# One layer of a hybrid attention and experts model: residual rows from transposed columns, two weight pieces held outside the ring

## The chip, the cores and the metric

The kernel runs on one core of a Trainium2 chip. The metric is device time in microseconds for one call, the median of several executions. The core has TensorE (PE) for matmuls, VectorE (DVE), ScalarE (ACT), GpSimd (POOL) and SyncE (SP), which here only issues DMAs.

## The reference

The input is 256 tokens of width 2048 in float32. After the projections, an attention, an mLSTM and an output projection, the layer ends like this:

```python
h = layer_norm(DN_ALPHA * h + mix @ w_out[l], ln1_g[l], ln1_b[l])
ff = hier_moe(h, w_grp[l], b_grp[l], w_exp[l], b_exp[l], w_gate[l], w_up[l], w_down[l])
ple = (p[l] @ w_ple[l]) * jax.nn.sigmoid(h @ w_ple_gate[l])
h = layer_norm(DN_ALPHA * h + ff + ple, ln2_g[l], ln2_b[l])
```

DN_ALPHA is 2 ** 0.25. There are 16 experts of hidden width 512 in 4 groups of 4; each token uses 2 experts of one group. The product h @ w_ple_gate is 256 x 2048 by 2048 x 2048.

## The kernel before

Up to about 934 us the kernel runs the projections. Each weight is split into a high and a low part, and four SBUF quarters of 1 MB are filled by SP. Then comes the first layer norm. DVE writes the normalised rows z (without gain and bias) into RES. PE transposes them (`row_turn`, L846), and ACT and DVE write the columns hT, with gain and bias, as h1T. The rows z also go to the output buffer in DRAM (L401), for a branch on overflow that is not taken here.

From about 965 us the experts run, in pairs: eight pairs, n = 0 to 7. `up(n)` (L999) has eight slots. A slot uses two loads of 1 MB, one for each expert of the pair, even slots from w_gate and odd ones from w_up (`up_slot`, L990, eight matmuls of 64 stationary columns by 512). `down(n)` (L1051) has four slots of two loads of w_down (`down_slot`, L1043). ORDER (L62) is up(0), up(1), down(0), up(2), down(1), up(3) and so on. PE also does, between slots: the gathers of the tokens of the next group (in up(0) and in down(0), down(2), down(4)), the turn of the hidden rows after slot 2 (`turn_pair`), and the scatters of pair n-2 after slots 2 and 5.

The product with w_ple_gate is cut into 16 chunks of 512 rows by 512 columns. The first (`ple_early`, loaded at L371) is held outside the ring and worked in up(0). The other 15, numbered i = 0 to 14, stand at the slots that CHUNKS_IN (L66) lists: after that slot, `ple_chunk` (L915) runs eight matmuls on one load of 1 MB. ACT copies the first chunk of four into ple_sig, DVE adds the others (`ple_added`, L2212).

All these weights come through moe_ring, 8 slots of 1 MB. The list LOADS (L84) holds its loads in the order of their use, each slot's two and behind them the chunk's one, 207 in all. SP issues them in this order (`ring_load`, L386). Load m goes into slot m % 8, and from m = 8 on SP waits for the use of load m - 8 (L393). So a load can't be issued while the ring is full, and nothing behind it either.

The residual rows are DN_ALPHA * h. Here ACT loads the gain and the bias of the first norm as broadcast rows (ln_g, ln_b, 1 MB each; at L1432 and L1433), scales both by ALPHA (L1590, L1591), and DVE multiplies and adds them to the rows of RES (`residual`, L2069 to L2076). ACT and DVE wait for that (res_ready) before the first sums of down(0).

Of the kernel before, what the change touches and what calls it, by code (L numbers as in the profile page):

```python
# [64 lines left out]

CHUNKS_IN = (("up", 1, 4), ("up", 2, 2), ("up", 2, 5), ("up", 3, 2), ("up", 3, 5), ("up", 4, 2), ("up", 4, 5),  # L66
             ("up", 5, 2), ("up", 5, 5), ("up", 6, 2), ("up", 6, 5), ("down", 5, 1), ("up", 7, 2), ("up", 7, 5),
             ("down", 6, 1))
SPLIT_FROM = 9
CHUNK_OF = {at: i for i, at in enumerate(CHUNKS_IN)}  # L70

# [13 lines left out]
for item in ORDER:  # L85
    for slot in range(SLOTS_OF[item[0]]):
        LOADS += [item + (slot, 0), item + (slot, 1)]
        if item + (slot,) in CHUNK_OF:
            LOADS.append(("ple", CHUNK_OF[item + (slot,)], 0, 0))
# [45 lines left out]
def build(nc, x, p, w_in, kv_norm, w_ukv, m_i_bias, m_f_bias, w_proj_a, w_proj_m, w_out, ln1_g, ln1_b,  # L135
          w_grp, b_grp, w_exp, b_exp, w_gate, w_up, w_down, w_ple, w_ple_gate, ln2_g, ln2_b, out):
    with ExitStack() as ctx:
# [21 lines left out]
        EW = at("ple_early", [EARLY, D], Z0 + 16384)  # L159
        lng = at("ln_g", [D], Z0)  # L160
        lnb = at("ln_b", [D], Z0 + 8192)
        ygh = at("yg_hi", [4, NC], Z0, F32R)
# [78 lines left out]
        def tiny(n):  # L241
# [49 lines left out]
        n2_diag, n2_mm, n2_out = sem("norm_diagonal"), sem("norm_mm"), sem("norm_out")  # L291
        z_ready, z_T, hT_act, hT_dve, rows_scaled = (sem("z_ready"), sem("z_T"), sem("hT_act"), sem("hT_dve"),
                                                     sem("rows_scaled"))
        wr_zero, r_part = sem("wr_zero"), sem("r_part")
        h1_hi, h1_lo, res_gain, res_ready = sem("h1_hi"), sem("h1_lo"), sem("res_gain"), sem("res_ready")
        ple_in, pT_mm, pT_c, pp_mm, pp_c = sem("ple_in"), sem("pT_mm"), sem("pT_copied"), sem("pp_mm"), sem("pp_copied")
        split_hi, split_lo = sem("turned_or_gate_hi"), sem("turned_or_gate_lo")
        z_moved = sem("z_rows_moved")
        ple_sig, ple_done, ple_ev = sem("ple_sig"), sem("ple_done"), sem("ple_evac")
        early_in, early_used = [sem(f"early_in{s}") for s in range(EARLY)], sem("early_used")  # L300
        r_in, r_row, r_mm, r_exp, r_log = sem("r_in"), sem("r_row"), sem("r_mm"), sem("r_exp"), sem("r_log")
# [25 lines left out]
        def _(sp):  # L327
# [42 lines left out]
            for q in range(EARLY):  # L370
                sp.dma_start(EW[:, EARLY - 1 - q, :].rearrange("p (t n) -> p t n", t=4),  # L371
                             ple_v[:, 4 * q:4 * q + 4, 0:NC]).then_inc(early_in[q], 16)
            load_tiles(T_OUT + 2, 2, w_out[0], 2 * NC)
            gate_v = w_gate.rearrange("l e (p t) f -> p (l e) t f", p=P)
            up_v = w_up.rearrange("l e (p t) f -> p (l e) t f", p=P)
# [140 lines left out]
        def _(pe):  # L516
# [398 lines left out]
            def ple_chunk(at, b):  # L915

                i = CHUNK_OF[at]
                pe.wait_ge(ple_ev, i + 1)
                if i < SPLIT_FROM:
                    ple_rows(landed_load(("ple", i, 0, 0)), b, (i + EARLY) % 4, True, True).then_inc(ring_used, 1)  # L920
                else:
                    split_rows(i, b).then_inc(ring_used, 1)
# [67 lines left out]
            def up_slot(w, i, b0, e0):  # L990
# [6 lines left out]
                return last  # L997

            def up(n):  # L999

                b, other = 2 * (n % 2), 2 * ((n + 1) % 2)
                if n and n % 2 == 0:
                    pe.wait_ge(g_act, 8 + 4 * (n // 2))
                    pe.wait_ge(g_dve, 4 * (n // 2))
                if n:
                    pe.wait_ge(ple_ev, max(chunks_in("up", n - 1) + chunks_in("down", n - 2), default=-1) + 2)
                for i in range(UP_SLOTS):
                    w = landed_pair("up", n, i)
                    if n == 0 and i % 2 == 0:
                        pe.wait_ge(g_act, i + 2)  # L1010
                    up_slot(w, i, b, 2 * (n % 2)).then_inc(ring_used, 2)
                    if n == 0 and i in (1, 3):
                        if i == 1:
                            pe.wait_ge(combined, 1)
                            weight_table(5, selT_mm)
                        first_pairs(i // 2 + 2)
                    if n == 0 and i == 6:
                        ple_rows(EW[:, 0, :], 2, 0, True, True, (1, 2, 3)).then_inc(early_used, 1)
                    if i == 2:
                        if n:  # L1020
# [174 lines left out]
        def _(ac):  # L1195
# [230 lines left out]
            def before(h):  # L1426
                if h < 3:
                    mix_turned(h + 3)
                if h == 4:
                    product(T_MIX + 15)  # L1430
                    ac.dma_start(RES[:], x[0].rearrange("(a p) k -> p a k", p=P)).then_inc(x2_in, 16)
                    ac.dma_start(lng[:], ln1_g[0:1, :].to_broadcast([P, D])).then_inc(ln_in, 16)  # L1432
                    ac.dma_start(lnb[:], ln1_b[0:1, :].to_broadcast([P, D])).then_inc(ln_in, 16)  # L1433
                    ac.dma_start(lgc, ln1_g[0].rearrange("(q t) -> q t", t=KT)).then_inc(ln_in, 16)
                    ac.dma_start(lbc, ln1_b[0].rearrange("(q t) -> q t", t=KT)).then_inc(ln_in, 16)
                    ac.dma_start(wple[:], w_ple[0].rearrange("(k p) n -> p k n", p=P)).then_inc(ple_in, 16)
                if h == 7:
                    mix_turned(6)
# [32 lines left out]
            for n in range(4):  # L1471
                pp_copy(n)
            ac.wait_ge(ln_in, 64)
            for i in range(0, 8, 2):
# [110 lines left out]
            for i in range(8):  # L1585
# [3 lines left out]
                gained(i, B[6 + i % 2]).then_inc(g_act, 1)  # L1589
            fn(lng[:], lng[:], ACT.Copy, scale=ALPHA).then_inc(rows_scaled, 1)  # L1590
            fn(lnb[:], lnb[:], ACT.Copy, scale=ALPHA).then_inc(rows_scaled, 1)  # L1591
            ple_started(0, 2)
            ac.wait_ge(r_all, 1)
            over = ac.value_load(flag[0:1, 0:1], min_val=0, max_val=1)
            for kind, n in ORDER:
                if kind == "up":
                    if n:
                        hidden_turned(n - 1)
                    if n >= 6:
                        gate_high(10 if n == 6 else 13)  # L1600
# [66 lines left out]
        def _(dv):  # L1667
# [400 lines left out]

            def residual(a):  # L2069

                dv.wait_ge(h1_lo, 4)
                dv.wait_ge(rows_scaled, 2)
                dv.wait_ge(z_moved, 16)
                v.tensor_tensor(RES[:, a, :], RES[:, a, :], lng[:], ALU.mult).then_inc(res_gain, 1)
                dv.wait_ge(res_gain, a + 1)
                v.tensor_tensor(RES[:, a, :], RES[:, a, :], lnb[:], ALU.add).then_inc(res_ready, 1)  # L2076

            moments(1, link)
            for a in range(NT):
                v.tensor_scalar(RES[:, a, :], RES[:, a, :], mv2[:, 2 * a:2 * a + 1], rstd[:, a:a + 1], ALU.subtract,  # L2080
                                ALU.mult).then_inc(z_ready, 1)
            dv.wait_ge(ln_in, 64)
            for i in range(1, 8, 2):
# [118 lines left out]
            def ple_part(j):  # L2202
# [3 lines left out]
                if j == 0:  # L2206
                    dv.wait_ge(pp_c, 8)
                    dv.wait_ge(res_ready, 2)
                link(v.tensor_tensor(psg[:], psg[:], pp[:, :, c], ALU.mult))
                v.tensor_tensor(RES[:, :, c], RES[:, :, c], psg[:], ALU.add).then_inc(ple_done, 1)  # L2210

            def ple_added(i, b):  # L2212

                dv.wait_ge(ring_used, LOAD_AT["ple", i, 0, 0] + 1)
                dv.wait_ge(ple_ev, i + 1)
# [28 lines left out]
            def add(n, c, b0, blocks=range(NT)):  # L2244

                if (n, c) == (0, 0):
                    dv.wait_ge(res_ready, 2)
                for a in blocks:
# [43 lines left out]
            overflow()  # L2292
            residual(0)
            residual(1)
            dv.wait_ge(r_all, 1)
            over = dv.value_load(flag[0:1, 0:1], min_val=0, max_val=1)
            for kind, n in ORDER[:-1]:
                for slot in range(SLOTS_OF[kind]):
                    if kind == "up" and n >= 2 and slot in (2, 5):
                        if parts_done((kind, n, slot)):  # L2300
# [146 lines left out]
```

## Time and profile before

| | us |
|---|---|
| median of 3 runs | 1511.32 |
| lowest and highest | 1510.46 and 1512.3 |
| the profiled execution | 1512.64 |
| its span, first to last instruction | 1511.1 |
| PE busy | 1481.9 (98%) |
| DVE busy | 701.2 (46%) |
| ACT busy | 513.5 (34%) |
| HBM read | 391.71 MB |

A busy PE is not PE at its peak, since the ends of matmuls are modelled. The chain that ended last gives PE 92% and DMA 4% of the span. An `L` number is a line of the kernel before. In a timeline, instructions of one kind in a row are merged, with their count behind an x; a bracket gives the idle time before and what ended it.

### The profile page before, as it was taken

To read this page: it belongs to the slowest core of one execution; us is meant where nothing else is said; L and a number is where in the kernel's file an instruction comes from. 1 tells how busy PE (TensorE), PEld (TensorE's weight loads), DVE (VectorE), ACT (ScalarE), POOL (GpSimd) and SP (SyncE) were. 2 spreads that over 40 slices of the span, in tenths; PEclk is the share of its full clock that TensorE was granted. 3 is DMA by queue.
4 is the path that set the end of the run, shared out by engine and by line. 5 is a ranking of instruction groups with operands and counts; after the bars stand their busy time and mean duration, and the time that the engine had idled before them with its cause. 6 is when DMAs were issued, how large, how long until landed. Compare 5 with 4: busy or idle time off the path is not lost.

```text
span 1511.1 us, 17027 instructions
## 1 busy us (share of the span) xinstructions
PE 1481.9 (98%) x6708; PEld 1012.9 (67%) x6708; DVE 701.2 (46%) x960; ACT 513.5 (34%) x690; POOL 55.1 (4%) x64
## 2 busy tenths in 40 slices
PE   9999999999999999999999999999999998999998
PEld 7887788888878888888888887534434443454443
DVE  5546665457746555454454655531221231143336
ACT  4444444454545443444444433521000200031111
POOL 0000000043300000000000000000000000000000
PEclk9999999999999999999999999999999999999999
DMA  8654555544444556555555876599999999999994
GB/s 307 198 173 161 167 168 195 192 151 159 139 141 138 176 172 202 192 191 189 193 193 191 312 263 228 202 418 421 416 416 417 396 389 421 419 388 419 416 403 177
DMA packets 133006, 397.00 MB, mean 263 GB/s; under 512 B 13248, under 2 KB 15936, under 8 KB 108096
## 3 DMA queue, kind: packets, MB, share of 16 engines
q1 hardware_dynamic: 124352, 388.65, 69.5%
q10 hardware_dynamic: 8576, 7.28, 1.5%
q8 instruction: 52, 0.85, 0.2%
q14 instruction: 26, 0.21, 0.0%
HBM read 391.71 MB, written 4.19 MB: 262 GB/s over the span
## 4 chain that ended last, share of the span: by engine, by line
PE 92%; DMA 4%; DVE 1%; issue 1%; ACT 1%; POOL 0%; SPq 0%; DVEq 0%; ACTq 0%; POOLq 0%
PE bank L525 19%; PE bank L526 19%; PE bank L530 19%; PE bank L995 12%; PE bank L1047 5%; PE bank L911 4%; DMA moe_ring<-in_w_gate_dram 2%; PE bank L959 2%; DMA moe_ring<-in_w_ple_gate_dram 2%; PE bank L1090 1%; PE bank L1075 1%; PE bank L1091 1%; PE bank L933 1%; PE bank L935 1%; PE bank L934 1%; DMA moe_ring<-in_w_down_dram 1%
## 5 line engine op out<-in xcount | busy, mean ns | idle before, releaser
L1681 DVE TENSOR_TENSOR w_lo<-w_ring,w_hi 128x1024 fp32r<-128x1024 f32 (+1 forms) x312 | 382.1, 1227 | 299.5 <-ACT w_hi L1211 298.4
L1211 ACT ACTIVATE w_hi<-w_ring 128x1024 fp32r<-128x1024 f32 (+1 forms) x312 | 327.3, 1051 | 308.0 <-PE bank L530 308.0
L525 PE MATMUL bank<-w_hi,xT_hi 128*128 128x512 f32 (+1 forms) x864 | 346.6, 401 | 1.7 <-ACT w_hi L1211 1.7
L526 PE MATMUL bank<-w_hi,xT_lo 128*128 128x512 f32 (+1 forms) x864 | 335.0, 388 | 0.0
L995 PE MATMUL bank<-moe_ring,xg 128*64 128x512 f32 x1024 | 225.9, 594 | 8.6 <-DMA moe_ring<-in_w_gate_dram 6.0
L530 PE MATMUL bank<-w_lo,xT_hi 128*128 128x512 f32 (+1 forms) x864 | 229.2, 387 | 0.0
L525 PEld LDWEIGHTS bank<-w_hi,xT_hi 128*128 128x128 f32 x864 | 162.3, 188 | 38.1 <-issue 6.7
L526 PEld LDWEIGHTS bank<-w_hi,xT_lo 128*128 128x128 f32 x864 | 162.5, 188 | 32.3 <-issue 1.9
L530 PEld LDWEIGHTS bank<-w_lo,xT_hi 128*128 128x128 f32 x864 | 161.6, 188 | 33.1
L995 PEld LDWEIGHTS bank<-moe_ring,xg 128*64 128x64 f32 x1024 | 72.7, 137 | 154.9 <-issue 154.5
L1047 PE MATMUL bank<-moe_ring,moe_hiddenT 128*64 128x512 f32 x448 | 100.0, 595 | 1.4 <-DMA moe_ring<-in_w_down_dram 1.4
L2254 DVE TENSOR_TENSOR res<-res,bank 128x512 f32<-128x512 f32 x62 | 38.5, 682 | 104.1 <-issue 80.0
L1047 PEld LDWEIGHTS bank<-moe_ring,moe_hiddenT 128*64 128x64 f32 x448 | 31.4, 137 | 61.2 <-issue 60.0
L911 PE MATMUL bank<-moe_ring,h1T 128*128 128x512 f32 x144 | 63.4, 593 | 0.0
L2217 DVE TENSOR_TENSOR ple_sig<-bank,ple_sig 128x512 f32<-128x512 f32 x24 | 15.5, 687 | 80.5 <-PE bank L911 57.1
L525 PE MATMUL bank<-w_hi,ymT_hi 128*128 128x512 f32 x128 | 50.4, 394 | 0.0
L525 PE MATMUL bank<-w_hi,mixT_hi 128*128 128x512 f32 x128 | 50.1, 391 | 0.0
L526 PE MATMUL bank<-w_hi,ymT_lo 128*128 128x512 f32 x128 | 49.9, 390 | 0.0
L526 PE MATMUL bank<-w_hi,mixT_lo 128*128 128x512 f32 x128 | 49.8, 389 | 0.0
L525 PE MATMUL bank<-w_hi,yaT_hi 128*128 128x512 f32 x128 | 49.8, 389 | 0.0
L526 PE MATMUL bank<-w_hi,yaT_lo 128*128 128x512 f32 x128 | 49.8, 389 | 0.0
L911 PEld LDWEIGHTS bank<-moe_ring,h1T 128*128 128x128 f32 x144 | 27.2, 190 | 31.6 <-issue 31.0
(297 smaller groups left out, 1390.9 us busy)
## 6 DMA issues: line engine op xcount, KB each, us to landing
w_ring<-in_w_in_dram SPq DMA_DIRECT2D x103, 1024.0 KB, 5.0
moe_ring<-in_w_gate_dram SPq DMA_DIRECT2D x64, 1024.0 KB, 9.7
moe_ring<-in_w_up_dram SPq DMA_DIRECT2D x64, 1024.0 KB, 10.4
moe_ring<-in_w_down_dram SPq DMA_DIRECT2D x64, 1024.0 KB, 10.3
w_ring<-in_w_proj_a_dram SPq DMA_DIRECT2D x16, 1024.0 KB, 5.0
w_ring<-in_w_proj_m_dram SPq DMA_DIRECT2D x16, 1024.0 KB, 5.0
w_ring<-in_w_out_dram SPq DMA_DIRECT2D x16, 1024.0 KB, 5.2
moe_ring<-in_w_ple_gate_dram SPq DMA_DIRECT2D x15, 1024.0 KB, 13.0
```

What stands on the lines that cost most here:

```text
L525: mm(b, lh(k, m), WH[:, s, kk, 0:width], start=start and kk == 0, stop=False)
L526: mm(b, ll(k, m), WH[:, s, kk, 0:width], start=False, stop=False)
L530: last = mm(b, lh(k, m), WL[:, s, kk, 0:width], start=False, stop=stop and kk == 1)
L911: ins = mm(B[b + a][:, :], hT[:, k, a * P:a * P + P], w[:, t * NC:t * NC + NC], start=first and t == 0, stop=last and t == 3)
L933: mm(B[b + a][:, :], hTh[:, k, r], GH[:, j % 2, c], start=t == 0, stop=False)
L959: last = mm(b[:, kk * TOK:kk * TOK + TOK], src[:, a, 2 * i + kk, :], selg[:, a, :], start=part == 0 and a == 0, stop=part == 1 and a == 1)
L995: last = mm(B[b0 + i % 2][CAP * e:CAP * e + CAP, :], xg[:, k, (e0 + e) * CAP:(e0 + e) * CAP + CAP], w[e][:, t * NC:t * NC + NC], start=k = ...
L1047: last = mm(B[4 + c][CAP * e:CAP * e + CAP, :], src[:, k, CAP * e:CAP * e + CAP], w[e][:, c * NC:c * NC + NC], start=k == 0, stop=k == 3)
L1211: fn(WH[:, h % 4, :, 0:width], W32[:, h // 2, 2 * (h % 2):2 * (h % 2) + 2, 0:width], ACT.Copy).then_inc(hi_ready, 1)
L1681: v.tensor_tensor(WL[:, h % 4, :, 0:width], W32[:, h // 2, 2 * (h % 2):2 * (h % 2) + 2, 0:width], WH[:, h % 4, :, 0:width].bitcast(F32), A ...
L2217: last = v.tensor_tensor(psg[:, a, :], B[b + a][:, :], psg[:, a, :], ALU.add)
L2254: v.tensor_tensor(r, r, B[b0 + a][:, :], ALU.add).then_inc(y_add, 1)
```

## The change

The residual rows are no longer made from the rows z. PE transposes the columns hT back, eight turns of four 128x128 blocks into banks 6 and 7, two turns after each of the slots 0, 1, 3 and 4 of up(1). ACT evacuates the even turns and DVE the odd ones, with the factor ALPHA, into the strided columns of RES. The broadcast rows, their loads and their scalings go. Their room holds the pieces of chunks 0 and 1, which SP loads behind the last tile of w_out and ahead of the ring's first load. The ring carries 205 loads. Chunk 0 moves from up(1) slot 4 to up(1) slot 2, chunk 1 from up(2) slot 2 to up(1) slot 4. A core of the diff:

```diff
-CHUNKS_IN = (("up", 1, 4), ("up", 2, 2), ("up", 2, 5), ("up", 3, 2), ("up", 3, 5), ("up", 4, 2), ("up", 4, 5),
+CHUNKS_IN = (("up", 1, 2), ("up", 1, 4), ("up", 2, 5), ("up", 3, 2), ("up", 3, 5), ("up", 4, 2), ("up", 4, 5),
...
+AHEAD = 2
...
-        if item + (slot,) in CHUNK_OF:
+        if CHUNK_OF.get(item + (slot,), -1) >= AHEAD:
             LOADS.append(("ple", CHUNK_OF[item + (slot,)], 0, 0))
...
-        lng = at("ln_g", [D], Z0)
-        lnb = at("ln_b", [D], Z0 + 8192)
+        AW = at("ple_ahead", [AHEAD, D], Z0)
...
             load_tiles(T_OUT + 2, 2, w_out[0], 2 * NC)
+            for q in range(EARLY, EARLY + AHEAD):
+                sp.dma_start(AW[:, q - EARLY, :].rearrange("p (t n) -> p t n", t=4),
+                             ple_v[:, 4 * q:4 * q + 4, 0:NC]).then_inc(early_in[q], 16)
...
-                if i < SPLIT_FROM:
+                if i < AHEAD:
+                    pe.wait_ge(early_in[EARLY + i], 16)
+                    ple_rows(AW[:, i, :], b, i + EARLY, True, True).then_inc(early_used, 1)
+                elif i < SPLIT_FROM:
...
+            def residual_turn(r):
+
+                pe.wait_ge(res_act if r % 2 == 0 else res_dve, r // 2)
+                for k in range(4):
+                    t, a = 4 * (r // 2) + k, r % 2
+                    last = nc.tensor.transpose(B[6 + a][:, k * P:k * P + P], hT[:, t, a * P:a * P + P], ident[:])
+                last.then_inc(res_T, 1)
...
                     up_slot(w, i, b, 2 * (n % 2)).then_inc(ring_used, 2)
+                    if n == 1 and i in (0, 1, 3, 4):
+                        for r in range(2):
+                            residual_turn(2 * (0, 1, 3, 4).index(i) + r)
...
                 if n:
                     pe.wait_ge(y_add, 2 * CHUNKS * n)
+                else:
+                    pe.wait_ge(res_act, 4)
+                    pe.wait_ge(res_dve, 4)
...
-                    ac.dma_start(lng[:], ln1_g[0:1, :].to_broadcast([P, D])).then_inc(ln_in, 16)
-                    ac.dma_start(lnb[:], ln1_b[0:1, :].to_broadcast([P, D])).then_inc(ln_in, 16)
...
-            fn(lng[:], lng[:], ACT.Copy, scale=ALPHA).then_inc(rows_scaled, 1)
-            fn(lnb[:], lnb[:], ACT.Copy, scale=ALPHA).then_inc(rows_scaled, 1)
...
+            def residual(r):
+
+                ac.wait_ge(h1_lo, 4)
+                ac.wait_ge(z_moved, 16)
+                ac.wait_ge(res_T, r + 1)
+                t = 4 * (r // 2)
+                fn(RES[:, r % 2, :].rearrange("p (q t) -> p t q", t=KT)[:, t:t + 4, :], four(6 + r % 2), ACT.Copy,
+                   scale=ALPHA).then_inc(res_act, 1)
+
             for kind, n in ORDER:
                 if kind == "up":
+                    if n == 1:
+                        residual(0)
+                        residual(2)
                     if n:
                         hidden_turned(n - 1)
+                    if n == 1:
+                        residual(4)
+                        residual(6)
...
                     if n == 0:
-                        ac.wait_ge(res_ready, NT)
+                        ac.wait_ge(early_used, EARLY + AHEAD)
...
-            def residual(a):
-
-                dv.wait_ge(h1_lo, 4)
-                dv.wait_ge(rows_scaled, 2)
-                dv.wait_ge(z_moved, 16)
-                v.tensor_tensor(RES[:, a, :], RES[:, a, :], lng[:], ALU.mult).then_inc(res_gain, 1)
-                dv.wait_ge(res_gain, a + 1)
-                v.tensor_tensor(RES[:, a, :], RES[:, a, :], lnb[:], ALU.add).then_inc(res_ready, 1)
...
             def ple_added(i, b):
 
-                dv.wait_ge(ring_used, LOAD_AT["ple", i, 0, 0] + 1)
+                if i < AHEAD:
+                    dv.wait_ge(early_used, EARLY + i + 1)
+                else:
+                    dv.wait_ge(ring_used, LOAD_AT["ple", i, 0, 0] + 1)
...
+            def residual(r):
+
+                dv.wait_ge(h1_lo, 4)
+                dv.wait_ge(z_moved, 16)
+                dv.wait_ge(res_T, r + 1)
+                t = 4 * (r // 2)
+                v.tensor_scalar(RES[:, r % 2, :].rearrange("p (q t) -> p t q", t=KT)[:, t:t + 4, :], four(6 + r % 2),
+                                ALPHA, None, ALU.mult).then_inc(res_dve, 1)
+
             for kind, n in ORDER[:-1]:
                 for slot in range(SLOTS_OF[kind]):
+                    if kind == "up" and n == 1 and slot in (0, 1, 3, 4):
+                        residual(2 * (0, 1, 3, 4).index(slot) + 1)
```

Every wait on ln_in is 32 and no longer 64, and the first `add` and the first `ple_part` wait for res_act and res_dve at 4 in place of res_ready at 2.

## Rows read from the trace of the kernel before

**Rows 1.** The page, 40 slices of the span: PE, DMA and GB/s.
```profile
PE   9999999999999999999999999999999998999998
...
DMA  8654555544444556555555876599999999999994
...
GB/s 307 198 173 161 167 168 195 192 151 159 139 141 138 176 172 202 192 191 189 193 193 191 312 263 228 202 418 421 416 416 417 396 389 421 419 388 419 416 403 177
```

**Rows 2.** Windows of the second stage: busy us (x count), PEclk, DMA share, GB/s.
```profile
970.00:1040.00 70.00, 69.10 (x308) 26.61 (x306) 14.54 (x18) 12.05 (x18) 0.00 (x0) 1.00 1.01 416
...
1040.00:1075.00 35.00, 34.71 (x189) 17.12 (x189) 6.47 (x12) 7.08 (x15) 0.00 (x0) 1.00 1.02 418
...
1190.00:1210.00 20.00, 19.87 (x102) 8.27 (x99) 4.47 (x8) 3.09 (x7) 0.00 (x0) 1.00 0.94 373
...
1220.00:1250.00 30.00, 30.00 (x124) 11.39 (x122) 9.37 (x19) 1.65 (x2) 0.00 (x0) 1.00 0.98 383
...
965.00:1485.00 520.00, 504.31 (x2239) 221.91 (x2239) 136.82 (x217) 75.40 (x124) 0.00 (x0) 1.00 1.00 406
```

**Rows 3.** Waits of PE after 850: us in total, times, longest us.
```profile
PE bank L995 <- DMA moe_ring<-in_w_gate_dram: 6.0, 5, 1.3
...
PE bank L995 <- DMA moe_ring<-in_w_up_dram: 2.6, 2, 1.3
...
PE bank L1047 <- DMA moe_ring<-in_w_down_dram: 1.4, 2, 0.9
```

**Rows 4.** Timeline of PE, 994 to 1060: start us, us, instructions merged.
```profile
999.90 13.95 PE L995 MATMUL bank<-moe_ring,xg 128*64 128x512 f32 x64
...
1013.78 0.66 PE L1036 MATMUL bank<-ident,moe_hidden 128*128 128x128 f32 x4
...
1014.37 7.09 PE L995 MATMUL bank<-moe_ring,xg 128*64 128x512 f32 x32
...
1021.39 7.13 PE L911 MATMUL bank<-moe_ring,h1T 128*128 128x512 f32 x16
...
1028.45 10.52 PE L995 MATMUL bank<-moe_ring,xg 128*64 128x512 f32 x48
...
1039.88 3.65 PE L1047 MATMUL bank<-moe_ring,moe_hiddenT 128*64 128x512 f32 x16 [0.90 <-DMA moe_ring<-in_w_down_dram]
...
1046.92 3.65 PE L1047 MATMUL bank<-moe_ring,moe_hiddenT 128*64 128x512 f32 x16
```

**Rows 5.** Timeline of SP's queue: first ring loads, first ones after a release.
```profile
909.12 7.47 SPq L394 DMA_DIRECT2D moe_ring<-in_w_gate_dram  x2
...
968.66 0.80 SPq L394 DMA_DIRECT2D moe_ring<-in_w_gate_dram  x2
```

**Rows 6.** Windows (columns as in Rows 2) before the experts' stage.
```profile
905.00:935.00 30.00, 30.00 (x134) 24.59 (x133) 13.24 (x14) 8.08 (x9) 0.53 (x1) 1.00 0.59 180
...
940.00:945.00 5.00, 4.70 (x33) 3.63 (x32) 3.66 (x7) 3.40 (x8) 0.00 (x0) 1.00 1.06 415
...
955.00:970.00 15.00, 14.29 (x79) 8.70 (x79) 11.80 (x33) 9.60 (x15) 0.00 (x0) 1.00 0.03 6
```

**Rows 7.** Groups by line and form, 880 to 1040: busy us, mean ns, idle before.
```profile
L858 PE MATMUL bank<-ident,res 128*128 128x128 f32 x32 | 4.0, 283 | 0.3 <-DVE res L2080 0.3
...
L2076 DVE TENSOR_TENSOR res<-res,ln_b 128x2048 f32<-128x2048 f32 x2 | 4.6, 2292 | 0.1
...
L2091 DVE TENSOR_TENSOR h_lo<-res,h_hi 128x512 fp32r<-128x512 f32 x8 | 8.0, 1086 | 0.0
...
L1571 ACT ACTIVATE moe_hiddenT<-bank 128x512 f32<-128x512 f32 x1 | 0.6, 597 | 11.5 <-PE bank L1036 11.5
```

**Rows 8.** Timeline of PE at the start of up(3), 1125 to 1136.
```profile
1125.60 3.65 PE L995 MATMUL bank<-moe_ring,xg 128*64 128x512 f32 x16 [1.21 <-DMA moe_ring<-in_w_gate_dram]
1130.57 3.65 PE L995 MATMUL bank<-moe_ring,xg 128*64 128x512 f32 x16 [1.32 <-DMA moe_ring<-in_w_up_dram]
1135.57 3.65 PE L995 MATMUL bank<-moe_ring,xg 128*64 128x512 f32 x16 [1.34 <-DMA moe_ring<-in_w_gate_dram]
```

More of the change, by code:

```diff
@@ L291, in build @@
         n2_diag, n2_mm, n2_out = sem("norm_diagonal"), sem("norm_mm"), sem("norm_out")
-        z_ready, z_T, hT_act, hT_dve, rows_scaled = (sem("z_ready"), sem("z_T"), sem("hT_act"), sem("hT_dve"),
-                                                     sem("rows_scaled"))
+        z_ready, z_T, hT_act, hT_dve, res_T = (sem("z_ready"), sem("z_T"), sem("hT_act"), sem("hT_dve"),
+                                               sem("res_T"))
         wr_zero, r_part = sem("wr_zero"), sem("r_part")
-        h1_hi, h1_lo, res_gain, res_ready = sem("h1_hi"), sem("h1_lo"), sem("res_gain"), sem("res_ready")
+        h1_hi, h1_lo, res_act, res_dve = sem("h1_hi"), sem("h1_lo"), sem("res_act"), sem("res_dve")
         ple_in, pT_mm, pT_c, pp_mm, pp_c = sem("ple_in"), sem("pT_mm"), sem("pT_copied"), sem("pp_mm"), sem("pp_copied")
@@ L299, in build @@
         ple_sig, ple_done, ple_ev = sem("ple_sig"), sem("ple_done"), sem("ple_evac")
-        early_in, early_used = [sem(f"early_in{s}") for s in range(EARLY)], sem("early_used")
+        early_in, early_used = [sem(f"early_in{s}") for s in range(EARLY + AHEAD)], sem("early_used")
         r_in, r_row, r_mm, r_exp, r_log = sem("r_in"), sem("r_row"), sem("r_mm"), sem("r_exp"), sem("r_log")
@@ L1472, in _ @@
                 pp_copy(n)
-            ac.wait_ge(ln_in, 64)
+            ac.wait_ge(ln_in, 32)
             for i in range(0, 8, 2):
@@ L2081, in _ @@
                                 ALU.mult).then_inc(z_ready, 1)
-            dv.wait_ge(ln_in, 64)
+            dv.wait_ge(ln_in, 32)
             for i in range(1, 8, 2):
@@ L2207, in ple_part @@
                     dv.wait_ge(pp_c, 8)
-                    dv.wait_ge(res_ready, 2)
+                    dv.wait_ge(res_act, 4)
+                    dv.wait_ge(res_dve, 4)
                 link(v.tensor_tensor(psg[:], psg[:], pp[:, :, c], ALU.mult))
@@ L2246, in add @@
                 if (n, c) == (0, 0):
-                    dv.wait_ge(res_ready, 2)
+                    dv.wait_ge(res_act, 4)
+                    dv.wait_ge(res_dve, 4)
                 for a in blocks:
@@ L2292, in _ @@
             overflow()
-            residual(0)
-            residual(1)
             dv.wait_ge(r_all, 1)
             over = dv.value_load(flag[0:1, 0:1], min_val=0, max_val=1)
+            def residual(r):
[5 more added lines that the diff above has]
+                                ALPHA, None, ALU.mult).then_inc(res_dve, 1)
             for kind, n in ORDER[:-1]:
                 for slot in range(SLOTS_OF[kind]):
+                    if kind == "up" and n == 1 and slot in (0, 1, 3, 4):
+                        residual(2 * (0, 1, 3, 4).index(slot) + 1)
                     if kind == "up" and n >= 2 and slot in (2, 5):
```

## The prediction

> **What bounds the kernel now.** I read the page's slices first. PE is busy in nearly every slice of the span. DMA is moderate up to the 26th slice and then sits at 9 tenths and about 418 GB/s until the end [rows 1]. So the span has two stages, and the change touches the second, the experts' stage from 965 us on. The windows say how tight it is: in 965 to 1485 the DMA engines are busy for 1.00 of the time and PE for 504.3 of 520 us, at clock 1.00 [rows 2]. Neither has spare room. What passes between them is the ring of 8 loads of 1 MB, where load m is issued only when load m-8 has been used (L393). A look at the waits shows PE short of ring loads for 6.0 + 2.6 + 1.4 = 10.0 us in all [rows 3]. The DMA is short of free slots elsewhere: it falls to 0.94 in 1190 to 1210 and to 0.98 in 1220 to 1250 [rows 2]. The reader is to see a system bound by turns. A pair slot (two loads) costs PE 13.95/4 = 3.49 us [rows 4] and the DMA twice 1.049 MB at 418 GB/s, that is 2 x 2.51 = 5.02 us. PE's other work (chunks, gathers, scatters) needs few loads and lets the DMA catch up. If too much of it stands together, the ring is full and the DMA idles; idle DMA time is lost for good, because the rest of the stage needs the DMA at 1.00.
>
> **The edits, part by part.**
>
> *Two ring loads go.* The ple pieces 0 and 1 are now loaded ahead. The ring carries two loads fewer: 2 x 2.51 = 5.0 us less DMA in the stage. They are issued on SP behind w_out's last tile and ahead of the ring's first load, which before was issued at 909.12 [rows 5]. In 905 to 935 the DMA share is 0.59, so 0.41 x 30 = 12.3 us are free against the 5.0 that come in, and in 955 to 970 the DMA stands still again (0.03) [rows 6]. The first ring loads are used at 965. I cost this at nothing; without that cover it would be 5.0 us. The two broadcast loads on ACT's queue (2 MB, around 880 us) go; PE has no wait there, so nothing is gained.
>
> *Residual rows.* Gone are four DVE operations of 128x2048, two of each of two lines, and two ACT scalings. One line's pair took 4.6 us, so the four are 9.2 us [rows 7]. All of it lies beside PE work and nothing on PE waits for it. Added are four evacuations on ACT and four on DVE of 128x512, between 0.60 us (a plain ACT evacuation) and 1.09 us (a DVE one with strided rows) [rows 7]. PE comes back to the same bank only after at least one slot of 3.49 us, so they are hidden. Cover gone, each costs up to 1.1 us. The new waits of ACT and DVE in up(1) stand ahead of the sigmoid, the hidden turn and the chunk sums; these are due one slot or more later. SP issues no DMA behind them.
>
> *Turns on PE.* Eight turns of four transposes enter up(1), two after each of slots 0, 1, 3 and 4. Thirty-two transposes in a row took 4.0 us [rows 7], four alone 0.6 us (1013.78 to 1014.37) [rows 4]. So all cost between 4.0 and 8 x 0.6 = 4.8 us. I take 4.4 (1.1 a visit), since they come in eights. They are on PE's path.
>
> The Trainium skill (TensorE: Matmul & The Clock Gate, Part 4: PE-mode transpose) gives about 275 ns for a 128x128 transpose in a kernel's context. Estimated from that page the turns would be 32 x 0.275 = 8.8 us, and the sum below about 4.4 us worse. The row with 32 of them speaks for 4.0 us, since they overlap.
>
> *Chunks move.* Chunk 0 moves from slot 4 to slot 2 of up(1), and chunk 1 from slot 2 of up(2) to slot 4 of up(1). A chunk costs PE 7.0 us (1021.39 to 1028.45) [rows 4]. Both now stand in up(1) with no load of their own in the ring. This is the part that decides.
>
> **The sum, by the ring.** I follow PE through up(1) from the timeline [rows 4]. Up(0) ends where four slots from 999.90 began, plus one: 1003.5. With 3.5 us a slot, 1.1 a visit, 0.6 for the turn of the hidden rows and 7.0 a chunk, slots 0 to 2 end at 1007.0, 1011.6 and 1016.2. The hidden turn and chunk 0 run to 1023.8. Slots 3 and 4 end at 1027.3 and 1031.9. The visit and chunk 1 run to 1040.0, and slots 5, 6, 7 end at 1043.5, 1047.0, 1050.5. Before, down(0) began at 1039.88, after a wait of 0.90 [rows 4]; so PE is 10.6 us late there.
>
> Now the DMA. Its stream starts about 970.4, some 1.5 us after the first release of 968.66 [rows 5], and takes 2.51 us a load. The release at 1016.2 has freed 22 loads, done at 970.4 + 22 x 2.51 = 1025.6. The next release is at 1027.3, transfers resume at 1028.8: 3.2 us lost. Slots 3 and 4 free four loads, done at 1038.8. The next release is 1043.5, resumed at 1045.0: 6.2 us lost. Slots 5 to 7 and the first three of down(0) (7.06 us each with a gather part, as from 1039.88 to 1046.92 [rows 4]) free 12 loads, done at 1075.1. The last slot of down(0) ends at 1075.3, resumed at 1076.8: 1.7 us lost. Together 11.1 us are lost, where before 970 to 1075 shows 1.01 and 1.02 with nothing lost [rows 2]. From there on up(2) has no chunk at slot 2, and its releases come faster than 5 us until slot 5, so the DMA runs through.
>
> Net: 11.1 lost less 5.0 saved is 6.1 us late at the loads of up(3). Before, PE waited there three times for them, and the third slot began at 1135.57 [rows 8]. PE's own path is only 4.4 + 0.1 a switch for 4 visits, less the wait of 0.90, about 3.9 us later there, so the DMA is what comes last: PE waits again, and for some 2 us more. From there both kernels do the same work in the same order, and the ring fills and empties as before: the delay is carried to the end. The turns count one for one in it, because they stand ahead of the releases. I take 6.0.
>
> The profiled execution took 1512.64 us with a span of 1511.1, that is 1.5 us around it, and the median of the three runs shown is 1511.32. A delay of 6.0 on the span adds the same to each: the forecast is 1511.3 + 6.0 = 1517.3 us.
>
> **The rivals.**
>
> 1. *The ring never runs full (faster).* If the DMA alone bounded the stage, two loads fewer would give 5.0 us back: 1506.3. For it speaks the DMA share of 1.00 over 520 us [rows 2]. Against it speaks the depth of the ring: 8 loads are 20 us of DMA, and in up(1) PE now spends 23.8 us (1016.2 to 1040.0) in which it frees only four loads. It would take a stream 5 us behind the one I worked out.
> [...]
>
> 2. *The turns go into PE's waits (no change).* PE's waits for loads up to the third slot of up(3) are 0.90 + 1.21 + 1.32 + 1.34 = 4.8 us [rows 4, 8]. If the DMA came 5 us earlier, the 4.4 of turns would fill them: -0.4 us, 1510.9. This needs the lost DMA time of up(1) to be under some 5 us.
>
> 3. *PE alone sets the delay (slower, less).* The DMA's lost time is smaller than 9 us and PE's extra path of 3.9 us shows: 1515.2.
>
> 4. *The turns cost more.* If each visit waits for an evacuation (up to 1.1 us), or the granted clock falls to the lower level of 1.2 GHz around them, up(1) grows by 4.4 us and the delay by the same: 1521.7. Against: in 940 to 945, which holds most of the 32 transposes of that row, the clock is 1.00 [rows 6].
> The Trainium skill (TensorE: Matmul & The Clock Gate, Part 4: PE-mode transpose) says that transposes don't count as PE work for the clock gate; here they make up 1.1 us between stretches of matmuls, and no row shows a fall after them.
>
> **Chances.** Forecast (delay of 4.5 to 8 us) 0.62; rival 3 (3 to 4.5) 0.12; rival 4 (over 8) 0.09; rival 2 (within 3 us) 0.11; rival 1, or another gain, 0.06. A measurement of this kernel can tell about 0.2% from no change, 3.0 us. So slower 0.83, same 0.11, faster 0.06. The range leaves out rivals 1 and 2 and the far end of rival 4: from 1511.3 + 2.7 = 1514.0 to 1511.3 + 9.2 = 1520.5.
>
> **What would show it.** In the profile after: PE's transposes of up(1) near 4.4 us in all; down(0) starting near 1050.5; the DMA share falling well below 1 in about 1025 to 1029 and 1039 to 1045; no wait of PE at the start of down(0); three or four waits of PE at the start of up(3), each near 1.3 us, with its third slot near 1141.6; and from there the same picture 6 us later. It would be wrong if the DMA is at 1.00 all through up(1), if the start of up(3) is not later than before, or if a new wait stands between a turn and its evacuation.

## The result and the profile after

| | before | changed |
|---|---|---|
| median of the timed runs, us | 1511.8 (6 runs) | 1517.14 (6 runs) |
| lowest and highest | 1509.52 and 1514.79 | 1516.18 and 1519.29 |
| profiled execution, us | 1512.64 | 1517.15 |
| its span | 1511.1 | 1515.6 |

The ratio is 1.0032, with a 95% interval of 1.0017 to 1.0046: the changed kernel is 0.3% slower, 5.3 us by the medians. 1517.3 was forecast. Further down, two of the ten executions of e7 (3904 and 5273 us) are left out of its numbers, and its trace is that of a second run, e7b.

The page of the changed kernel, the lines that answer to [rows 1] (span; 40 slices of PE, of the DMA engines, and the GB/s moved):

```profile
span 1515.6 us, 17099 instructions
...
PE   9999999999999999999999999999989998999997
...
DMA  9654555554443555555565867597999999999994
...
GB/s 308 199 182 148 169 174 193 187 167 139 140 159 124 188 167 194 194 194 194 194 194 192 314 216 273 217 421 316 402 422 416 386 398 421 418 389 419 416 403 175
```

PE is as full as before. The DMA is not: the 28th slice, which begins at 27 x 37.9 = 1023 us, has fallen to 7 tenths and 316 GB/s. That slice covers the second half of up(1) and the start of down(0).

PE's timeline there, as in [rows 4] (start us, us, instructions merged, count):

```profile
1006.12 1.09 PE L1010 MATMUL bank<-ident,h1T 128*128 128x128 f32 x8
...
1007.15 3.65 PE L1001 MATMUL bank<-moe_ring,xg 128*64 128x512 f32 x16
...
1010.73 1.09 PE L1010 MATMUL bank<-ident,h1T 128*128 128x128 f32 x8
...
1015.34 0.66 PE L1053 MATMUL bank<-ident,moe_hidden 128*128 128x128 f32 x4
...
1015.83 7.03 PE L914 MATMUL bank<-ple_ahead,h1T 128*128 128x512 f32 x16
...
1026.38 1.09 PE L1010 MATMUL bank<-ident,h1T 128*128 128x128 f32 x8
...
1030.99 1.09 PE L1010 MATMUL bank<-ident,h1T 128*128 128x128 f32 x8
...
1031.92 7.03 PE L914 MATMUL bank<-ple_ahead,h1T 128*128 128x512 f32 x16
...
1038.88 10.52 PE L1001 MATMUL bank<-moe_ring,xg 128*64 128x512 f32 x48
...
1049.23 3.60 PE L1064 MATMUL bank<-moe_ring,moe_hiddenT 128*64 128x512 f32 x16
```

L1010 are the turns, L914 the chunks, L1053 the turn of the hidden rows, L1064 down(0). Eight transposes take 1.03 us of PE (1006.12 to 1007.15). Chunk 0 stands at 1015.83, chunk 1 at 1031.92. Down(0) begins at 1049.23 and no longer waits for a load; before it began at 1039.88 after a wait [rows 4]. The whole stage began 0.8 us earlier in this profiled execution. That comes from the first 10 us of the kernel, where the eight transposes that begin at 5.92 took 1.07 us in place of 1.91, in a part that the change doesn't touch.

Windows of 5 us (busy us of PE, PEld, DVE, ACT, POOL with counts, granted clock, DMA share, GB/s):

```profile
1015.00:1020.00 5.00, 5.00 (x16) 2.40 (x15) 0.00 (x0) 0.60 (x1) 0.00 (x0) 1.00 1.02 426
...
1020.00:1025.00 5.00, 5.00 (x19) 1.73 (x18) 1.29 (x2) 0.00 (x0) 0.00 (x0) 1.00 0.89 372
...
1025.00:1030.00 5.00, 5.00 (x28) 2.05 (x26) 1.04 (x1) 1.05 (x1) 0.00 (x0) 1.00 0.51 172
...
1030.00:1035.00 5.00, 5.00 (x22) 2.48 (x19) 1.03 (x1) 1.03 (x1) 0.00 (x0) 1.00 1.02 413
...
1035.00:1040.00 5.00, 5.00 (x16) 1.93 (x16) 1.01 (x2) 0.00 (x0) 0.00 (x0) 1.00 0.63 262
...
1040.00:1045.00 5.00, 5.00 (x26) 1.64 (x24) 0.28 (x1) 0.00 (x0) 0.00 (x0) 1.00 0.27 75
...
1045.00:1050.00 5.00, 5.00 (x26) 1.66 (x24) 1.25 (x2) 0.60 (x1) 0.00 (x0) 1.00 1.01 423
...
1070.00:1075.00 5.00, 5.00 (x26) 1.82 (x26) 1.28 (x3) 1.01 (x3) 0.00 (x0) 1.00 0.80 328
...
1075.00:1080.00 5.00, 5.00 (x26) 1.72 (x24) 2.20 (x4) 1.15 (x3) 0.00 (x0) 1.00 0.98 383
```

Here the lost DMA time can be counted against a full rate of 421 GB/s, which most full windows of 5 us reach within 1%. In 1020 to 1030 it is (49 + 249)/421 x 5 = 3.5 us. In 1035 to 1045 it is (159 + 346)/421 x 5 = 6.0 us, and in 1070 to 1080 (93 + 38)/421 x 5 = 1.6 us. Together 11.1 us, in just the three places of the forecast (3.2, 6.2 and 1.7).

The start of up(3), as in [rows 8]:

```profile
1125.04 3.65 PE L1064 MATMUL bank<-moe_ring,moe_hiddenT 128*64 128x512 f32 x16 [1.31 <-DMA moe_ring<-in_w_down_dram]
...
1130.02 3.65 PE L1001 MATMUL bank<-moe_ring,xg 128*64 128x512 f32 x16 [1.33 <-DMA moe_ring<-in_w_gate_dram]
...
1135.00 3.65 PE L1001 MATMUL bank<-moe_ring,xg 128*64 128x512 f32 x16 [1.32 <-DMA moe_ring<-in_w_up_dram]
...
1139.97 3.65 PE L1001 MATMUL bank<-moe_ring,xg 128*64 128x512 f32 x16 [1.32 <-DMA moe_ring<-in_w_gate_dram]
```

PE waits there four times, 5.3 us in all. Before it waited 0.90 at down(0) and 3.9 in up(3) [rows 4, 8]. To compare stages I count from the start of the second gather group, 962.89 before and 962.10 now, to the third slot of up(3): 172.7 us before, 177.9 now. The delay is 5.2 us, and it is all made by then. From that slot to the last sums (the first L1130 before, L1150 now) it is 355.2 us before and 354.8 now.

### The profile page after: what moved, and what is told of

Its sections match the earlier page's. It is cut to its first block, busy times and chain, and to the rows that moved or that the text cites. A ratio compares the mean times of both kernels' runs of the same rounds, so it can differ in the third digit from the quotient of the medians.

```text
span 1515.6 us, 17099 instructions
## 1 busy us (share of the span) xinstructions
PE 1485.5 (98%) x6740; PEld 1015.3 (67%) x6740; DVE 695.9 (46%) x960; ACT 513.7 (34%) x692; POOL 55.0 (4%) x64
## 4 chain that ended last, share of the span: by engine, by line
PE 93%; DMA 4%; DVE 1%; issue 1%; ACT 1%; POOL 0%; SPq 0%; DVEq 0%; POOLq 0%; ACTq 0%
PE bank L528 19%; PE bank L529 19%; PE bank L533 19%; PE bank L1001 13%; PE bank L1064 5%; PE bank L914 4%; DMA moe_ring<-in_w_gate_dram 2%; PE bank L965 2%; DMA moe_ring<-in_w_ple_gate_dram 2%; PE bank L1110 1%; PE bank L1095 1%; PE bank L1111 1%; PE bank L939 1%; PE bank L940 1%; PE bank L941 1%; PE bank L555 1%
## 5 line engine op out<-in xcount | busy, mean ns | idle before, releaser
L528 PEld LDWEIGHTS bank<-w_hi,xT_hi 128*128 128x128 f32 x864 | 162.3, 188 | 37.9 <-issue 4.6
L1064 PE MATMUL bank<-moe_ring,moe_hiddenT 128*64 128x512 f32 x448 | 100.4, 595 | 1.8 <-DMA moe_ring<-in_w_down_dram 1.7
L1064 PEld LDWEIGHTS bank<-moe_ring,moe_hiddenT 128*64 128x64 f32 x448 | 31.5, 137 | 61.7 <-issue 60.5
L914 PE MATMUL bank<-moe_ring,h1T 128*128 128x512 f32 x112 | 49.2, 592 | 0.0
L2267 DVE TENSOR_TENSOR yg_lo<-bank,yg_hi 128x512 fp32r<-128x512 f32 x32 | 20.1, 682 | 50.4 <-ACT yg_hi L1596 49.9
```

The costliest lines, as they stand in the source:

```text
L528: mm(b, lh(k, m), WH[:, s, kk, 0:width], start=start and kk == 0, stop=False)
L914: ins = mm(B[b + a][:, :], hT[:, k, a * P:a * P + P], w[:, t * NC:t * NC + NC], start=first and t == 0, stop=last and t == 3)
L1064: last = mm(B[4 + c][CAP * e:CAP * e + CAP, :], src[:, k, CAP * e:CAP * e + CAP], w[e][:, c * NC:c * NC + NC], start=k == 0, stop=k == 3)
L2267: v.tensor_tensor(ygl[:, c, :], B[c if n == NP - 1 else 4 + c][:, :], ygh[:, c, :].bitcast(F32), ALU.subtract).then_inc(y_lo, 1)
```

## The experiments

"Stage" is the time from the second gather group to the third slot of up(3) in the profiled execution, less the 172.7 us of before. Each is read from one execution. The other columns are timed runs against the kernel before on the same chip. The ratio isn't the quotient of the two medians; the two differ most for e7 (4.4 us by the ratio, 2.7 by the medians).

| kernel | stage, us | median, us | before, us | ratio and 95% interval |
|---|---|---|---|---|
| changed | +5.2 | 1517.14 | 1511.8 | 1.0032 (1.0017 to 1.0046) |
| e1_no_turns | +0.9 | 1511.87 | 1512.87 | 0.9997 (0.9988 to 1.0006) |
| e2_in_ring | +6.2 | 1518.32 | 1512.87 | 1.0034 (1.0022 to 1.0047) |
| e3_chunks_moved | +1.5 | 1512.37 | 1512.87 | 0.9994 (0.9985 to 1.0003) |
| e4_one_ahead | +5.4 | 1515.94 | 1512.87 | 1.0020 (1.0008 to 1.0031) |
| e7_spare_turns_up1 | +5.3 | 1515.16 | 1512.41 | 1.0029 (1.0016 to 1.0042) |
| e8_spare_turns_down1 | +1.6 | 1512.26 | 1512.41 | 1.0000 (0.9990 to 1.0010) |
| e5_spread | | 1509.4 | 1512.41 | 0.9980 (0.9969 to 0.9991) |
| e9_after_spread | | 1511.36 | 1512.41 | 0.9999 (0.9990 to 1.0008) |
| e10_spread_in_ring | | 1512.4 | 1511.77 | 0.9999 (0.9990 to 1.0008) |

(In the last three a chunk stands inside the stretch, so the stage is not comparable. The stage of e7 is that of e7b, the same kernel.)

### Without the turns: e1_no_turns

The calls of residual_turn and of residual on ACT and DVE are taken out of the changed kernel; DVE's first sums wait for z_moved. DN_ALPHA * h is left out: the sums are added to the rows z.

```diff
-                    if n == 1 and i in (0, 1, 3, 4):
-                        for r in range(2):
-                            residual_turn(2 * (0, 1, 3, 4).index(i) + r)
...
-                    dv.wait_ge(res_act, 4)
-                    dv.wait_ge(res_dve, 4)
+                    dv.wait_ge(z_moved, 16)
```

> The changed kernel without the eight turns of the residual columns and without their evacuations; DN_ALPHA * h is left out, the sums are added to the rows z. Ring theory (a delay is made of DMA time lost while the ring is full, less 5.0 us for two loads saved): slots of up(1) are released earlier by 1.1 us a visit, so lost DMA time falls from about 10 to about 6.7 us (1.0 + 4.0 + 1.7) and the kernel is 1 to 2 us slower than before. Rival (PE's own path alone sets the delay): the two chunks only move past each other, 0 to -1 us against before. Rival (the turns are hidden in PE's waits): still 5 us slower.

The whole loss is gone: 0.9997. In the trace the stage is 0.9 us longer than before. So the turns with their evacuations, of which 4.4 us are PE's, are worth 4.3 us of stage and about 5 us of time, give or take 2.6: they are not hidden. The expected 1 to 2 us slower was not seen in the timed runs; the interval reaches 0.9 us. Why the stage's 0.9 us doesn't show there stays open, as for e3 below.

### The two pieces in the ring again: e2_in_ring

```diff
-AHEAD = 2
+AHEAD = 0
```

> The changed kernel with pieces 0 and 1 loaded through the ring again (207 ring loads), all else as changed. Ring theory: the two loads fall into time in which the DMA stands idle because the ring is full, so nothing changes against the changed kernel: 5 to 6 us slower than before, and the idle DMA time of up(1) is 5 us shorter. Rival (each ring load costs its 2.5 us of DMA in a stage with DMA share 1.00): 5 us more than the changed kernel, 10 us slower than before.

1.0034 against the changed kernel's 1.0032: two loads more cost nothing that the timing shows, and 1.0 us of stage. The windows show where they went (same columns as above):

```profile
1015.00:1035.00 20.00, 20.00 (x79) 8.45 (x76) 3.36 (x4) 2.69 (x3) 0.00 (x0) 1.00 1.01 397
...
1035.00:1055.00 20.00, 20.00 (x90) 7.95 (x89) 2.73 (x4) 1.44 (x4) 0.00 (x0) 1.00 0.90 357
```

The changed kernel has 346 and 297 GB/s in these two windows, this one 397 and 357. That is (51 + 60) GB/s x 20 us = 2.2 MB more: the two loads have filled idle DMA time. The rule that every load counts 2.5 us in a stage with DMA share 1.00 fell.

### Only the chunks moved: e3_chunks_moved

```diff
-CHUNKS_IN = (("up", 1, 4), ("up", 2, 2), ("up", 2, 5),
+CHUNKS_IN = (("up", 1, 2), ("up", 1, 4), ("up", 2, 5),
```

This is the kernel before, with ring loads for all chunks.

> The kernel before with chunks 0 and 1 at up(1) slots 2 and 4, nothing else. Ring theory: PE spends one chunk more in up(1), the ring is full for part of it, and this stage's DMA loses more than the two loads take: 1 to 2 us slower than before. Rival (position is free as long as the order of work is kept): 0.

The stage grew by 1.5 us, as expected, but the timed runs say 0.9994, a miss: no loss of 1 to 2 us. The traces show one thing that goes the other way. Near the end, in the last split chunk, the granted clock fell in the profiled executions of before, changed, e2 and e4, and not in those of e1 and e3. It is worth 1.6 us (the last section has the rows). In the timed runs it doesn't make up the difference: the mean clock that they list is 0.9981 for e3 and 0.9978 for before, and in before's runs 0.001 of it goes with some 0.9 us (1511.65 us on average at 0.999, 1513.32 at 0.997), so this gives 0.2 us. Why the stage's 1.5 us doesn't show in the timed runs stays open.

### One piece ahead, the chunks at their old places: e4_one_ahead

```diff
-CHUNKS_IN = (("up", 1, 2), ("up", 1, 4), ("up", 2, 5),
+CHUNKS_IN = (("up", 1, 4), ("up", 2, 2), ("up", 2, 5),
...
-AHEAD = 2
+AHEAD = 1
```

> The changed kernel with one piece ahead and both chunks at their old places, up(1) slot 4 and up(2) slot 2; the turns stay. Ring theory: 3.5 to 4.5 us slower than before, so the move of the chunks is worth 1 to 2 of the change's 5 us and the turns the rest. Rival (the clump of chunks and turns is all of the cost): 0 to 1 us slower than before.

1.0020, or 3.0 us, with an interval from 1.2 to 4.7 us; the stage is 5.4 us longer, more than the expected 4.5 and as much as the changed kernel's. So, in the stage, the clump of chunks and the second load ahead together carry nothing that the turns don't carry already. The timed runs are 1.8 us below the changed kernel's by the ratios, which their intervals don't tell from nothing. The idle DMA time is only spread differently:

```profile
1035.00:1040.00 5.00, 5.00 (x26) 1.73 (x24) 0.00 (x0) 0.41 (x1) 0.00 (x0) 1.00 0.66 220
...
1065.00:1070.00 5.00, 5.00 (x26) 1.61 (x24) 1.72 (x4) 2.06 (x4) 0.00 (x0) 1.00 0.74 272
```

(220 and 272 GB/s of 421 are 2.4 and 1.8 us lost; 2 us more are lost in 1105 to 1115.)

### The same PE work in two places: e7_spare_turns_up1 and e8_spare_turns_down1

Both are the kernel before with 32 spare transposes of hT into banks that nobody reads. They differ only in the place.

```diff
+            def spare_turn(bank, r):
+                for k in range(4):
+                    t, a = 4 * (r // 2) + k, r % 2
+                    nc.tensor.transpose(B[bank][:, k * P:k * P + P], hT[:, t, a * P:a * P + P], ident[:])
...
                     up_slot(w, i, b, 2 * (n % 2)).then_inc(ring_used, 2)
+                    if n == 1 and i in (0, 1, 3, 4):
+                        for a in range(2):
+                            spare_turn(6 + a, 2 * (0, 1, 3, 4).index(i) + a)
```

and for e8

```diff
                     down_slot(w, k, hidT[:, n % 2]).then_inc(ring_used, 2)
+                    if n == 1:
+                        if k == 0:
+                            pe.wait_ge(ple_ev, max(chunks_in("up", 2)) + 2)
+                        for a in range(2):
+                            spare_turn(2 + a, 2 * k + a)
```

> The kernel before with 32 spare transposes of hT on PE after slots 0, 1, 3 and 4 of up(1), into banks 6 and 7, read by nobody; chunks, loads and residual rows as before. If PE's time in up(1) is what the change pays for, this alone is 4 to 5 us slower than before, as the changed kernel is. Rival (the evacuations and their waits, or the moved chunks, carry the cost): 0 to 1 us.

> The same kernel as e7_spare_turns_up1, for a look at its trace. By the ring theory the DMA share falls below 1 somewhere in 1035 to 1085 by some 4 us in all, PE's waits at the start of up(3) stay at 1.3 us each, and its third slot starts 4 to 5 us later after the start of the ring slots than before. By the rival (PE's own path) the DMA share stays at 1 and the waits shrink.

> The kernel before with the same 32 spare transposes, now two turns after each slot of down(1), into banks 2 and 3, just ahead of the three waits of 1.2 to 1.3 us for ring loads at the start of up(3). If the price of PE work depends on where it stands in the ring's cycle, those waits shrink by most of the 4.4 us and the kernel is 0 to 1.5 us slower than before. Rival (PE work of this stage costs its own time anywhere): 4 to 5 us slower.

In up(1) the transposes alone cost 1.0029, which is 4.4 us of 1512.4 (interval 2.4 to 6.4): as much as the changed kernel loses, within the intervals, with no evacuation, no new wait and no moved chunk. In down(1) the same 32 transposes cost nothing that the timed runs show: 1.0000, with an interval of 1.5 us each way. The third slot of up(3) in e7b:

```profile
1130.51 3.65 PE L995 MATMUL bank<-moe_ring,xg 128*64 128x512 f32 x16 [1.32 <-DMA moe_ring<-in_w_gate_dram]
...
1135.49 3.65 PE L995 MATMUL bank<-moe_ring,xg 128*64 128x512 f32 x16 [1.33 <-DMA moe_ring<-in_w_up_dram]
...
1140.46 3.65 PE L995 MATMUL bank<-moe_ring,xg 128*64 128x512 f32 x16 [1.32 <-DMA moe_ring<-in_w_gate_dram]
```

PE still waits its 1.3 us per slot: the DMA is late. Where it lost its time:

```profile
1065.00:1070.00 5.00, 5.00 (x26) 1.71 (x24) 1.80 (x3) 2.07 (x4) 0.00 (x0) 1.00 0.86 320
...
1090.00:1095.00 5.00, 5.00 (x26) 1.73 (x24) 0.00 (x0) 0.00 (x0) 0.00 (x0) 1.00 0.97 372
...
1105.00:1110.00 5.00, 5.00 (x22) 1.70 (x22) 2.42 (x3) 1.06 (x1) 0.00 (x0) 1.00 0.94 341
...
1110.00:1115.00 5.00, 5.00 (x27) 1.59 (x24) 3.44 (x10) 0.60 (x1) 0.00 (x0) 1.00 0.88 336
```

That is 1.2 + 0.6 + 0.9 + 1.0 = 3.7 us against 421 GB/s, and 0.3 at 1085 to 1090. Expected were some 4 us in 1035 to 1085; the amount is right, the place is mostly later, in up(2), which holds two chunks and two scatter groups. The stage is 5.3 us longer, and before lost 0.6 us too, so this count leaves almost 2 us of the delay unexplained. In e8, PE's waits at the start of up(3) shrink to one of 0.21 us, where there were 3.9 [rows 8]:

```profile
1136.01 3.65 PE L995 MATMUL bank<-moe_ring,xg 128*64 128x512 f32 x16 [0.21 <-DMA moe_ring<-in_w_gate_dram]
```

```profile
1100.00:1140.00 40.00, 39.79 (x189) 15.04 (x188) 8.87 (x18) 3.72 (x6) 0.00 (x0) 1.00 0.99 404
```

PE is busy for 39.8 of 40 us where it was 36.1 before:

```profile
1100.00:1140.00 40.00, 36.13 (x159) 12.75 (x158) 8.88 (x18) 3.87 (x7) 0.00 (x0) 1.00 1.01 414
```

The work has taken the place of the waits, if not wholly: the stage of e8 is 1.6 us longer than before.

### Chunks moved out of the full-ring stretch: e5_spread, e9_after_spread, e10_spread_in_ring

```diff
-CHUNKS_IN = (("up", 1, 4), ("up", 2, 2), ("up", 2, 5), ("up", 3, 2), ("up", 3, 5), ("up", 4, 2), ("up", 4, 5),
-             ("up", 5, 2), ("up", 5, 5), ("up", 6, 2), ("up", 6, 5), ("down", 5, 1), ("up", 7, 2), ("up", 7, 5),
+CHUNKS_IN = (("up", 1, 4), ("up", 2, 2), ("up", 2, 5), ("up", 2, 7), ("up", 3, 2), ("up", 4, 2), ("up", 4, 5),
+             ("up", 4, 7), ("up", 5, 2), ("up", 6, 2), ("up", 6, 5), ("down", 5, 1), ("up", 7, 2), ("up", 7, 5),
```

e5 is the kernel before with that. e9 is the changed kernel with the same two moves, and e10 is e9 with AHEAD = 0.

> The kernel before with two chunks moved: the one at up(3) slot 5 to up(2) slot 7, and the one at up(5) slot 5 to up(4) slot 7 (the same 15 chunks in the same order, 207 ring loads). They leave the stretch in which the ring is full (DMA share 0.94 at 1190 to 1210, 0.86 at 1330 to 1340) and stand ahead of the stretch in which PE waits for loads. Ring theory: 2 to 3.5 us faster than before. Rival (the DMA's or PE's total alone counts, both unchanged): 0.

> The changed kernel with the same two chunks moved in the same way. Ring theory: it gains as much or more than the kernel before does by that, 2.5 to 4.5 us against the changed kernel, so 1 to 2.5 us slower than before. Rival: no change against the changed kernel, 5 us slower than before.

> The changed kernel with the two later chunks spread (e9_after_spread) and with pieces 0 and 1 through the ring again (207 ring loads). Ring theory: the two loads still fall into the idle DMA time of up(1), so it stays within 1 us of e9_after_spread, about as fast as before. Rival (now that the later stage no longer loses DMA time, each load counts 2.5 us): 3 to 5 us slower than e9_after_spread.

e5 is 0.2% faster than before, 3.0 us by the medians (interval 1.4 to 4.7 us): the fastest kernel of the study, with no work or load taken away. The windows where the ring was full read, before:

```profile
1180.00:1210.00 30.00, 29.71 (x162) 14.48 (x161) 6.46 (x12) 6.30 (x13) 0.00 (x0) 1.00 0.96 389
...
1320.00:1340.00 20.00, 19.71 (x110) 10.11 (x108) 7.32 (x10) 8.91 (x14) 0.00 (x0) 1.00 0.92 362
```

and in e5:

```profile
1180.00:1210.00 30.00, 29.71 (x161) 14.44 (x161) 6.47 (x12) 6.23 (x13) 0.00 (x0) 1.00 1.02 417
...
1320.00:1340.00 20.00, 19.71 (x109) 9.84 (x109) 9.12 (x13) 8.90 (x14) 0.00 (x0) 1.00 1.01 409
```

The traces bear this out only in part. From the second gather group to the first of the last sums it is 527.9 us before, 532.6 in the changed kernel, 527.3 in e9, 527.1 in e10 and 527.4 in e5. So e9 and e10 gain some 5 us on the changed kernel in the trace as well, but e5's profiled execution gains only 0.5 us. It was the second slowest of e5's twelve and had two falls of the granted clock (0.66 in 1385 to 1390, 0.71 in 1455 to 1460) where before's had one on this way. That the filled windows give the 3.0 us of the timed runs is not shown.

e9 is as fast as before (0.9999), so it gained some 5 us on the changed kernel; expected were 2.5 to 4.5. e10, with two loads more, is at 0.9999 too (by the medians, each against its own before, it is 1.7 us behind e9): the rival named for e10, that each load counts 2.5 us once the later stretch is mended, fell as well. The two loads fall into the idle time of up(1), which these moves don't touch.

## Why the prediction was right

*The sum.* Forecast 6.0 us of delay and 1517.3 us; measured 5.2 us in the stage, 5.3 us by the medians, 1517.14 us. The DMA time lost in up(1) and down(0) was 11.1 us where 11.1 was worked out, and at 1020, 1035 and 1070 us. Of the difference of 0.8 us, 0.6 can be put to time that the kernel before lost too and the changed one doesn't:

```profile
1105.00:1110.00 5.00, 5.00 (x26) 1.64 (x24) 3.11 (x3) 1.65 (x2) 0.00 (x0) 1.00 0.96 367
```

PE waits longer at the start of up(3), as said, but by 1.4 us (5.3 against 3.9) and not by some 2.

*Two ring loads go.* Right in size (2 x 2.5 us of DMA) and in the cover for their new place. The two loads were issued at 903.70 and held the ring's first one back by nothing (908.34 here, 909.12 before [rows 5], with the whole execution 0.8 us early):

```profile
903.70 0.93 SPq L375 DMA_DIRECT2D ple_ahead<-in_w_ple_gate_dram  x2
...
908.34 7.46 SPq L397 DMA_DIRECT2D moe_ring<-in_w_gate_dram  x2
```

The DMA share of 905 to 935 rose from 0.59 [rows 6] to 0.76, which is 0.17 x 30 = 5.1 us. And e2 and e10 show that what they save is worth nothing that the timing shows, and 1.0 us of stage, where the sum took off 5.0: with the two loads in the ring the DMA loses that much less. Rival 1 (1506.3) fell with that.

*Residual rows.* The evacuations cost nothing on PE, as said. Each took 1.03 to 1.04 us, near the upper end of the bound, on both engines. (The row behind the 1.09, L2091 in [rows 7], is no evacuation of a bank: it reads res and h_hi.) Groups, with busy us, mean ns and idle before:

```profile
L1010 PE MATMUL bank<-ident,h1T 128*128 128x128 f32 x32 | 4.4, 280 | 0.0
...
L1617 ACT ACTIVATE res<-bank 128x512 f32<-128x512 f32 x4 | 4.2, 1040 | 22.4 <-PE bank L1010 22.4
...
L2328 DVE TENSOR_SCALAR res<-bank 128x512 f32<-128x512 f32 x4 | 4.1, 1030 | 12.9 <-PE bank L1010 12.9
```

*Turns.* 4.4 us of PE forecast, 4.4 measured as busy time (L1010 above), and 4.0 from the start of each visit to the start of what follows it (1.03 us for the first). Their price counts one for one, or a little more: 4.3 us of stage by e1, 4.4 us of time and 5.3 of stage by e7. The Trainium skill (TensorE: Matmul & The Clock Gate, Part 4: PE-mode transpose) gives about 275 ns for one 128x128 transpose in bf16. In this trace, in float32, the mean duration of a record is near it, 280 ns. The records overlap, so it is no price: eight took 1.03 us. Rival 4 fell: no turn waited, and the clock was 1.00 in up(1).

*Chunks move.* Here a remark failed, and not the sum. "This is the part that decides" was said of the two chunks, though the sum itself charges 4.4 of its 6.1 us to the turns. e3 gives it 1.5 us of stage and nothing in the timed runs, and e4, with the chunks at their old places, keeps the stage's delay in full. What decides is the 4.4 us of PE work of the turns: e7, which has only them, makes the whole delay of the stage. The chunks' clump (0.9 us, from e7's 5.3 to e2's 6.2) and the two loads saved (1.0 us, from e2's 6.2 to 5.2) about cancel. Without the turns the ring's sum is 6.7 - 5.0, some 1.7 us, of which 0.9 showed (e1).

*Rival 2 and rival 3.* Rival 2 (the turns go into PE's waits) is not what up(1) does, but it is just what happens in down(1), as e8 shows but for its 1.6 us of stage: its mechanism was real and its place was wrong. Rival 3 (PE's own path, 3.9 us) is near the measured delay. Its condition, less than 9 us of lost DMA time, wasn't met (11.1), and it is told apart by the waits: PE waits 5.3 us in the changed kernel and 5.5 us in e7b for loads before the third slot of up(3), where that rival lets the waits shrink.

*From there the same picture.* Right within 0.4 us.

## What to carry to other kernels

In this kernel a ring of loads couples PE and the DMA, both full, and the price of a piece of PE work depends on the stretch: where the work leads to a full ring it delays the releases and costs its time (e7), and just ahead of a stretch in which PE waits for loads it costs little or nothing (e8). Look for both kinds of stretch in windows of 5 us before you add, move or remove work. The two loads saved ahead of a stretch where the ring is full brought nothing that the timing shows, and moving two chunks out of such a stretch brought more (e5 and e9).

## What was not expected

The granted clock. Just before the last split chunk PE waits 2.0 to 2.4 us for its high and low parts in every profile. Then the clock fell in some executions and not in others. Changed kernel: start of the chunk, start of the last sums, and the window of 5 us that holds the fall:

```profile
1458.64 0.47 PE L939 MATMUL bank<-gate_hi,h1T_hi 128*128 128x512 f32 x1 [2.38 <-DVE gate_lo L2302]
...
1494.74 0.50 PE L1150 MATMUL bank<-yg_hi,moe_selT 128*128 128x512 f32 x1 [0.35 <-DVE yg_lo L2267]
...
1460.00:1465.00 5.00, 5.00 (x17) 3.93 (x16) 0.00 (x0) 0.00 (x0) 0.00 (x0) 0.66 1.02 396
```

The kernel with only the chunks moved (e3):

```profile
1456.18 0.47 PE L933 MATMUL bank<-gate_hi,h1T_hi 128*128 128x512 f32 x1 [2.40 <-DVE gate_lo L2275]
...
1490.66 0.50 PE L1130 MATMUL bank<-yg_hi,moe_selT 128*128 128x512 f32 x1 [0.35 <-DVE yg_lo L2241]
...
1460.00:1465.00 5.00, 5.00 (x25) 2.42 (x25) 1.97 (x3) 1.06 (x1) 0.00 (x0) 1.00 1.04 386
```

Both waited 2.4 us. The first got a mean clock of 0.66 over the 5 us, which means the lower level of 1.2 GHz for part of it, and took 36.10 us from the chunk to the last sums. The second stayed at 2.4 GHz and took 34.48 us. The kernel before fell as well:

```profile
1455.00:1460.00 5.00, 5.00 (x17) 3.93 (x16) 0.00 (x0) 0.00 (x0) 0.00 (x0) 0.66 1.00 397
```

All eleven profiles split in this way: 36.07 to 36.12 us in the eight where the clock fell, 34.48 or 34.49 in e1, e3 and e7b. So 1.6 us of difference between two executions can come from this alone, as much as the effect looked for in e1 and e3. What sets it is open. The length of the wait alone doesn't: it was 1.99 us before, where the clock fell, and 2.40 in e3, where it did not. In e1 the clock fell at an earlier split chunk (0.66 in 1390 to 1395, after a wait of 2.61 us), and that chunk with the slots behind it took some 0.5 us longer than before.
